# Expert stage in 64-row sub-tiles, two on TensorE's column halves, with expert weights in a ring; front and combine rearranged

## What is computed

```python
h = rmsnorm(x, norm1_w) * (1 + sc1) + sh1          # sh1, sc1, ... = split(silu(c) @ w_ada + b_ada, 6)
x = x + g1 * mixer(h)                              # includes the S5 scan and h @ w_gate
h = rmsnorm(x, norm2_w) * (1 + sc2) + sh2
# each row goes to 2 of 16 experts: the best group of 4, then the best two inside it
for e in range(16):
    he = silu(hf @ w_exp_gate[e]) * (hf @ w_exp_up[e])      # 1024 -> 256
    out = out + combine[:, e:e + 1] * (he @ w_exp_down[e])  # 256 -> 1024
y = rmsnorm(x + g2 * out, final_norm_w)
```

## Time and profile before

| | us |
|---|---|
| median of 3 runs | 2274.26 (2273.16 to 2274.49) |
| the profiled execution | 2273.5 |
| its span (first to last instruction) | 2270.9 |
| TensorE matmuls busy | 2074.7 (91%) |
| VectorE / ScalarE / POOL busy | 708.1 / 398.6 / 187.9 |
| moved by DMA | 245.71 MB |

### The profile page before, as it was taken

How to read it: one execution, slowest core, us unless ns; L and a number is a source line. 1 busy time by engine, 2 the same in 40 slices (tenths; PEclk the granted TensorE clock), 3 DMA queues, 4 the chain that set the end, 5 groups by cost and what they waited for, 6 DMA issues and landing times. The chain is left out here.

```text
span 2270.9 us, 26307 instructions
## 1 busy us (share of the span) xinstructions
PE 2074.7 (91%) x10412; PEld 1408.4 (62%) x10412; DVE 708.1 (31%) x1540; ACT 398.6 (18%) x851; POOL 187.9 (8%) x226
## 2 busy tenths in 40 slices
PE   6998499999989999997899999899999399999976
PEld 3674275654456665654789898566444388778852
DVE  3737701202052112333344444311232411111117
ACT  4220111003132001222212122300111111111102
POOL 2000000000000001210212121100000000000016
PEclk9999799999999999998999999999999599999988
DMA  8085331110021000110000000212200299999975
GB/s 283 30 145 204 130 89 37 41 37 0 0 52 29 28 28 20 37 37 1 19 11 11 1 11 19 95 42 102 88 38 28 79 358 345 357 354 352 353 245 190
DMA packets 187757, 245.71 MB, mean 108 GB/s; under 512 B 25583, under 2 KB 155143, under 8 KB 185575
## 3 DMA queue, kind: packets, MB, share of 16 engines
q1 hardware_dynamic: 179080, 214.51, 30.0%
q0 software_dynamic: 8592, 30.01, 3.7%
HBM read 212.28 MB, written 31.04 MB: 107 GB/s over the span
## 5 line engine op out<-in xcount | busy, mean ns | idle before, releaser
L2581 PEld LDWEIGHTS ex_ps<-ex_xt,ex_w_in 128*128 128x128 f32 x2048 | 235.1, 193 | 17.7 <-issue 14.8
L2581 PE MATMUL ex_ps<-ex_xt,ex_w_in 128*128 128x128 f32 x2048 | 235.4, 276 | 2.5 <-DMA ex_w_in<-in_w_exp_up 2.5
L1471 PE MATMUL cv_ps<-h,late 128*128 128x364 f32 (+1 forms) x576 | 179.0, 474 | 2.7 <-PEq L2821 2.7
L1471 PEld LDWEIGHTS cv_ps<-h,late 128*128 128x128 f32 x576 | 110.5, 193 | 70.4 <-issue 6.6
L2226 PE MATMUL pj_ps<-w_out,mix 128*128 128x512 f32 (+1 forms) x288 | 125.0, 593 | 2.8 <-PEq L2821 2.8
L2075 PE MATMUL go_ps<-h,out_w 128*128 128x364 f32 (+1 forms) x384 | 122.2, 473 | 4.1 <-PEq L2821 4.1
L2592 PE MATMUL ex_ps<-ex_w_down,ex_hid 128*128 128x512 f32 x256 | 118.2, 605 | 6.5 <-DVE ex_hid L2667 4.3
L1263 PE MATMUL gla_ps<-h,early 128*128 128x364 f32 (+1 forms) x384 | 120.7, 469 | 0.0
L459 PE MATMUL fr_ps<-h,fr_w_gate 128*128 128x364 f32 (+1 forms) x384 | 120.1, 471 | 0.0
L2075 PEld LDWEIGHTS go_ps<-h,out_w 128*128 128x128 f32 x384 | 73.8, 192 | 48.7 <-issue 5.6
L459 PEld LDWEIGHTS fr_ps<-h,fr_w_gate 128*128 128x128 f32 x384 | 72.1, 190 | 48.9 <-issue 7.6
(11 more groups left out here) (471 smaller groups left out, 2776.0 us busy)
## 6 DMA issues: line engine op xcount, KB each, us to landing
ex_w_in<-in_w_exp_gate SPq DMA_DIRECT2D x32, 1024.0 KB, 8.6
ex_w_in<-in_w_exp_up SPq DMA_DIRECT2D x32, 1024.0 KB, 11.2
ex_w_down<-in_w_exp_down SPq DMA_DIRECT2D x32, 1024.0 KB, 10.2
fr_y_cols<-in_w_ada SPq DMA_DIRECT2D x8, 2048.0 KB, 7.6
ys_dram<-ex_y SPq DMA_DIRECT2D x32, 512.0 KB, 10.1
late<-in_w_in SPq DMA_DIRECT2D x12, 512.0 KB, 4.4
glu_w_br<-in_w_ada SPq DMA_DIRECT2D x5, 1024.0 KB, 5.7
mix<-in_x_prompt SPq DMA_DIRECT2D x8, 512.0 KB, 10.8
```

Of the source, the lines that this page charges most:

```text
L1471: last = nc.tensor.matmul(ps[n][:, 0:width], g.cv_w(j % 2)[:, k], g.h[:, k, at:at + width], start=k == 0, stop=k == KD - 1)
L2581: last = nc.tensor.matmul(ps[2 + b][:, P * m:P * m + P], w_in[:, b, m // 2, k, P * (m % 2):P * (m % 2) + P], xt[:, b, k], start=m == 0 and ...
```

## The change

The expert stage is rewritten. The list is padded to 64 places for each expert instead of 128. There are 50 sub-tiles in 25 slots; sub-tile A of a slot uses columns 0 to 63 of TensorE's array and sub-tile B columns 64 to 127. The rows are now stationary (128x64) and the weights move (256 and 512 columns), and the matmuls of A and B alternate, each pair writing the two halves of the partitions of one PSUM bank. The product then has its rows on partitions and is transposed (two transposes and a copy) before down. Each expert's weights are loaded once, in order of experts, to a ring of four places; the first four loads stand in the route stage, later ones wait for the slot that last used the place. TensorE takes A's weights from the ring at an address from a register; B's are copied each slot to fixed buffers, by ScalarE (two of the eight row blocks of gate/up, and down) and VectorE (six row blocks). The y buffer is single and is stored from POOL's queue. POOL also makes the 18 diagonal matrices for the combine meanwhile. In the combine, VectorE adds to x instead of POOL. In the front, there are five slab buffers, all x tiles are turned before the first modulation, the placement in `s5_toeplitz` is issued by POOL, `EARLY` is 6, the late slabs are used at every second piece, and SP's order is changed.

The diff, cut to its core:

```diff
 # front
-        slabs = [glu_space[:, 0:2 * D], br_space[:, 0:2 * D], br_space[:, 2 * D:4 * D]]
+        slabs = [glu_space[:, 0:2 * D], br_space[:, 0:2 * D], br_space[:, 2 * D:4 * D], s_space[:, 2 * D:4 * D], b_space[:, 2 * D:4 * D]]
-        EARLY = 5
+        EARLY = 6
-            for l in range(LB):        # SP
-                sp.dma_start(g.s5_toeplitz[...], lags[:, :, 0:LB - l, :]).then_inc(placed, 16)
+            pool.wait_ge(lags_done, 1)  # POOL
+            for l in range(LB):
+                pool.dma_start(g.s5_toeplitz[...], lags[:, :, 0:LB - l, :]).then_inc(placed, 16)
+            late(1)
             gate_weights(2)
-            late(1)
             late(2)
             gate_weights(3)
             late(3)
             late(4)
             gate_weights(4)
             late(5)
-            late(6)
             gate_weights(5)
+            late(6)
             late(7)
+            gate_weights(6)
...
-            for i in range(5):
+            for i in range(NT):
                 turn_x(i)
             for k in range(4):
                 modulation(k)
-                turn_x(5 + k)
...
-                if q % 3:
-                    late(q - 1 - q // 3)
+                if q % 2 and q < 15 or q == 14:
+                    late(q // 2)
 # route
-            then(nc.vector.tensor_scalar(tiles[:, 0], total[:, NT], 0.0, None, ALU.is_gt))
-            for j in range(1, NT):
-                then(nc.vector.scalar_tensor_tensor(tiles[:, j % 2], total[:, NT], float(P * j), tiles[:, (j - 1) % 2], ALU.is_gt, ALU.add))
+            then(nc.vector.tensor_scalar(tiles[:, 0], total[:, NT], 1.0, float(SUB - 1), ALU.max, ALU.add))
+            then(nc.vector.tensor_copy(tiles_i[:, 0], tiles[:, 0]))
+            then(nc.vector.tensor_scalar(tiles_i[:, 1], tiles_i[:, 0], 6, None, ALU.logical_shift_right))
+            then(nc.vector.tensor_copy(tiles[:, 1], tiles_i[:, 1]))
+            for e in range(RING):      # SP, in the route stage
+                if e:
+                    sp.wait_ge(g.experts_loaded, 48 * e)
+                load_expert(sp, g, d, e)
 # experts, SP
+            for e in range(RING, NE):
+                after = sp.value_load(g.free_at[0:1, e - RING:e - RING + 1], min_val=2, max_val=2 * SLOTS)
+                sp.wait_ge(g.experts_loaded, 48 * e)
+                sp.wait_ge(S["down_psum"], after)
+                load_expert(sp, g, d, e)
 # experts, POOL
+            for s in range(SLOTS):
+                if s + 2 < SLOTS:
+                    pool.wait_ge(S["high_turned"], s + 1)
+                    gather(s + 2)
+                if 1 <= s <= NT:
+                    weights_of(s - 1)
+                pool.wait_ge(S["y_out"], 2 * s + 2)
+                pool.dma_start(g.ys_dram[P * s:P * s + P, :], y[:]).then_inc(S["stored"], 16)
 # experts, TensorE
+            def gate_up(s, place):
+                pe.wait_ge(S["xt_out"], 2 * s + 2)
+                pe.wait_ge(S["in_copied_act"], s + 1)
+                pe.wait_ge(S["in_copied_dve"], s + 1)
+                if s:
+                    pe.wait_ge(S["inner"], s)
+                for f, (bank, done) in enumerate(((gate_ps, "gate_psum"), (up_ps, "up_psum"))):
+                    for k in range(KD):
+                        own = g.ring[:, place, FF * (2 * k + f):FF * (2 * k + f) + FF].rearrange("p r f -> p (r f)")
+                        nc.tensor.matmul(bank[A, 0:FF], xt[:, s % 2, k, A], own, start=k == 0, stop=k == KD - 1, ...)
+                        last = nc.tensor.matmul(bank[B, 0:FF], xt[:, s % 2, k, B], lane_in[:, s % 2, k, f], start=k == 0, stop=k == KD - 1, ...)
+                    last.then_inc(S[done], 1)
+            def down(s, place):
+                ...
+                for c in range(2):
+                    for k in range(FF // P):
+                        nc.tensor.matmul(down_ps[c][A], inner_t[:, k, A], own, ...)
+                        last = nc.tensor.matmul(down_ps[c][B], inner_t[:, k, B], lane_down[:, k, 512 * c:512 * c + 512], ...)
+                    last.then_inc(S["down_psum"], 1)
+            for s in range(SLOTS):
+                place = bass.ds(pe.value_load(g.ring_of[0:1, 2 * s:2 * s + 1], min_val=0, max_val=RING - 1), 1)
+                need = pe.value_load(g.need[0:1, 2 * s:2 * s + 1], min_val=48, max_val=48 * NE)
+                pe.wait_ge(g.experts_loaded, need)
+                gate_up(s, place)
+                if s + 1 < SLOTS:
+                    turn_low(s + 1)
+                turn_inner(s)
+                if s + 1 < SLOTS:
+                    turn_high(s + 1)
+                down(s, place)
 # experts, ScalarE
+            for s in range(SLOTS):
+                copy_down(s, place)
+                if s + 1 < SLOTS:
+                    place = place_of(s + 1)
+                    copy_in(s + 1, place)
+                ...
 # experts, VectorE
+            for s in range(SLOTS):
+                if s:
+                    store_half(s - 1)
+                if s + 1 < SLOTS:
+                    copy_in(s + 1)
+                ...
 # combine
-                pool.wait_ge(S["gated"], 2 * i + 2)
-                nc.gpsimd.tensor_tensor(x1[0:n, i], x1[0:n, i], gated[0:n, i % 2], ALU.add).then_inc(S["added"], 1)
+                dve.wait_ge(S["gated"], 2 * i + 2)
+                nc.vector.tensor_tensor(x1[0:n, i], x1[0:n, i], gated[0:n, i % 2], ALU.add).then_inc(S["added"], 1)
```

More of the change, by code:

```diff
@@ L163, in stage_front @@
         x_in = [sem(f"x_in{i}") for i in range(NT)]
-        slab_in = [sem(f"slab_in{b}") for b in range(3)]
+        slab_in = [sem(f"slab_in{b}") for b in range(5)]
         pad_zero = sem("pad_zero")
@@ L2427, in _ @@
             groups, experts = g.logits[:, :, 0:NG], g.logits[:, :, NG:]
-            then(nc.vector.tensor_tensor_scan(count[:], g.ones[:, 0:MT], g.ones[:, 0:MT], 0.0, ALU.mult, ALU.add))
+            then(nc.vector.tensor_tensor_scan(count[:], g.ones[:, 0:SUBS], g.ones[:, 0:SUBS], 0.0, ALU.mult, ALU.add))
             then(nc.vector.tensor_scalar(rank[:], count[:, 0:NE], -1.0, NE + 1.0, ALU.mult, ALU.add))
@@ new lines, in weights_of @@
+            def weights_of(i):
+                n = P if i < NT - 1 else DEC
+                for k in range(2):
+                    nc.gpsimd.tensor_scalar(g.diag(i, k)[0:n, 0:n], g.ident[0:n, 0:n], g.choice_w[0:n, k, i:i + 1], None, ALU.mult).then_inc(g.diag_made, 1)
+            gather(0)
+            gather(1)
+            for s in range(SLOTS):
[6 more added lines that the diff above has]
+                pool.dma_start(g.ys_dram[P * s:P * s + P, :], y[:]).then_inc(S["stored"], 16)
@@ L2585, in down, with turn_low @@
-            def down(t, b, rounds, freed):
-                pe.wait_ge(down_loaded[b], rounds)
-                pe.wait_ge(S["hid"], t + 1)
-                if freed is not None:
-                    pe.wait_ge(S["y_out"], freed)
+            def turn_low(s):
+                pe.wait_ge(x_loaded[s % 2], 16 * (s // 2 + 1))
+                if s:
+                    pe.wait_ge(S["xt_out"], 2 * s)
+                for k in range(4):
+                    last = nc.tensor.transpose(low_ps[:, P * k:P * k + P], x[:, s % 2, P * k:P * k + P], g.ident[:])
+                last.then_inc(S["low_turned"], 1)
@@ L2611, in _ @@
-            down(t, 0, 8 * MT, 2 * t - 2)
-            gate_up(t + 1, 1, 16 * MT, t)
-            down(t + 1, 1, 8 * MT, 2 * t)
+                        at = 2 * KD * FF + D * k + 512 * c
+                        own = g.ring[:, place, at:at + 512].rearrange("p r f -> p (r f)")
+                        nc.tensor.matmul(down_ps[c][A], inner_t[:, k, A], own, start=k == 0, stop=k == FF // P - 1, skip_group_check=True)
+                        last = nc.tensor.matmul(down_ps[c][B], inner_t[:, k, B], lane_down[:, k, 512 * c:512 * c + 512], start=k == 0,
+                                                stop=k == FF // P - 1, skip_group_check=True)
@@ L2714, in stage_combine @@
         rstd = sb("rstd", [P, NT])
-        S = {n: sem(n) for n in "gathered0 gathered1 gathered2 gains_loaded weights psum gated added ssq std rstd y stored".split()}
+        S = {n: sem(n) for n in "gathered0 gathered1 gathered2 gains_loaded psum gated added ssq std rstd y stored".split()}
         gathered = [S[f"gathered{b}"] for b in range(3)]
@@ L2735, in _ @@
                 gather(i)
[L2736 to L2741 removed]
+            for i in range(3, NT):
+                gather(i)
         @block.sync
@@ L2765, in _ @@
                     for k in range(2):
-                        last = nc.tensor.matmul(ps[2 * (i % 2) + c][0:n], weights[0:n, i % 2, k, 0:n], rows[0:n, i % 3, k, 512 * c:512 * c + 512],
+                        last = nc.tensor.matmul(ps[2 * (i % 2) + c][0:n], g.diag(i, k)[0:n, 0:n], rows[0:n, i % 3, k, 512 * c:512 * c + 512],
                                                 start=k == 0, stop=k == 1)
@@ L2780, in _ @@
         def _(dve):
-            def weigh(i):
-                n = size(i)
-                if i >= 2:
```

(4 more changed lines are left out.)

354 lines of the change are left out of this document (166 added, 188 removed).

## The result

The changed kernel takes 2182.35 us (median, 2181.19 to 2188.91), the kernel before 2274.02 in the same comparison: a ratio of 0.960, 95% interval 0.958 to 0.962, 92 us less. The forecast was 2176 in 2157 to 2248. The profiled execution took 2183.2 us with a span of 2181.4, 89.5 less than before.

| from one event to the next (us) | before | after | gain | forecast |
|---|---|---|---|---|
| start to the gated linear unit (front) | 346.70 | 331.83 | 14.87 | 14.5 |
| to the last logits (unchanged stages) | 1427.30 | 1424.57 | 2.73 | 0 |
| to the first listing product (route) | 19.91 | 18.75 | 1.16 | 1.1 |
| to the end of `row_token` | 8.59 | 8.53 | 0.06 | 0 |
| to the first gather of rows | 1.00 | 10.39 | **-9.39** | 0 |

The account below looks back on a forecast made before the run. TensorE was taken to set the experts' pace, loads just keeping up. Gains 69.3 (experts) + 1.65 (route, start) + 12 (combine) + 14.5 (front) = 97.4 us, from 2273.5 to 2176 us, range 2157 to 2248.

Parts of the forecast that it names:

- Halves: Experts, TensorE: matmul pairs alternating between the two column halves overlap at half price, 0.1105 us per 256-column record.
- one after the other: Rival, gate/up and down pairs: the halves run serially, 10.5 us more a slot, total 2440 us; chance 0.06.
- overlap in part: Rival, expert pairs: 1.25 passes each, 2.6 us more a slot, total 2242 us; chance 0.18, shared with a late copy.
- The slot: Experts: 25 slots of 12.45 us each replace 32 tiles; gain 69.3 us, bounds 85 and 43.
- The chain: Experts, between gate/up and down: product, two transposes, PSUM copy and four hops take 1.71 us, against 1.0 to 1.2 before.
- The DMA share: Experts: loads fall from 96 to 48 MB, 141 of 313 us at 340 GB/s; share near 0.5, off the path.
- Registers: Rival, experts: run-time addresses of 20 matmuls a slot cost 152 us if none were hidden, total 2328 us; chance 0.04.
- The copies: Experts, B's weights: ScalarE 1.9 + 1.0 us and VectorE 2.3 us a slot, covered by gate/up.
- Route and start: Route compares -1.1 us, first gate/up -1.55 us, last store some 1 us slower: net gain 1.65, bounds 0 and 3.
- The last store: End of the experts: POOL's issue of the last y store is some 1 us slower.
- Combine: VectorE's period falls from 5.53 to 4.08 us with the add on VectorE: gain 12 us, bounds 6 (late gathers) and 14.
- Front: EARLY=6 moves a gate column into the 27.08 us scan wait: gain 14.5 us, bounds 5 and 17; failure rival 2186 us, 0.10.

Follow-up runs that it names:

- my experiment: The changed kernel with the last of the 25 stores of expert outputs issued by SyncE instead of GpSimd: 2180.36 us, ratio 0.959.
- GpSimd experiment: The changed kernel with the combine's residual addition on GpSimd again, its weights still made beforehand: 2192.69 us.
- gains experiment: The changed kernel with three route loads, last store on SyncE, and the combine's gains and norm weights loaded one slot before the experts end: 2166.99 us.
- the kernel with seven columns: The changed kernel with seven gate columns ahead of the S5 outputs instead of six (EARLY = 7): 2192.8 us in one execution.
- blocks of two: The changed kernel with gate and up products in the order A, A, B, B instead of A, B: 2182.98 us.

## Why the forecast held, step by step

**Halves.** Half price for alternating pairs was taken from the S5 inputs, 136 columns wide; it holds at 256 columns (0.216 us a pair) and at 512 (down's 16 records, 6.9 us at 0.434 each, take 3.65 with their drain). The rivals "one after the other" and "overlap in part" had no share. The figure of the Trainium skill's TensorE: Matmul & The Clock Gate, section Part 3: Packing small matmuls, that I had set against it (2.38 for three column tiles), does not carry over to two halves: measured, two.

**The slot.** 12.45 forecast, 12.24 measured; the gain of 69.3 became 72.3. The chain was right to 0.02 us, the pairs 2% cheaper than the line between two full-width forms. The first slot took 2.7 us more than the others, where 1.5 were forecast. The DMA share was 0.59 and not near 0.5: the 141 us of loads left out the gathers and the y stores (and took 1 MB as 10^6 bytes; with the 3.15 MB of one expert's three matrices it is 148). Registers cost nothing that shows: pairs follow each other without gaps. The copies are covered, as costed (1.76 to 1.99 us on VectorE, 2.3 in the sum; 1.9 and 1.05 on ScalarE).

**Route and start.** Here the sum failed. Compares (1.16) and start (1.56) are right, but the step on the loads ("They now wait on SP for the down of the slot that frees a place") looked only at the experts. The first four loads I moved into the route's block without costing their queue: 3 MB at a time, each waiting for the one before, 11.05 us apart, so SyncE reaches the barrier 9.2 us after the list is ready. I had read them only as weights that are there in time, and left out that the block ends with its slowest engine. Part of the price was to be had from rows of before: three experts are 9.44 MB, 27.8 us at 340 GB/s. With two figures of after, 2.5 us for the fourth's issue (1790.46 to 1792.93) and 26.4 from the first load to the list, that is 30.3 us against 26.4, 4 us late. Measured, it was 9.2, since a load whose landing is waited for takes 11.05 us and not 9.25.

**The last store.** "POOL's issue of the last store is some 1 us slower" named the right instruction and priced the wrong thing. From the end of the issue to the first gather pass 7.6 us on GpSimd and 3.3 on SyncE, for the same 512 KB. The landing is not the difference (2.9 and 2.6 us from the start of the issue), though my experiment was built on it, and its 4.45 us came out right by luck. The term that was missing is GpSimd's DRAIN behind the last store: 4.16 us in all seven kernels that store from GpSimd to the end, 4.07 and off the path in the four others, 0.007 on SyncE. Why it takes that long stays open. Of 25 stores only the last is exposed.

**Combine.** 12 and 12.2, for the reason given: 9.7 of it is the addition (GpSimd experiment). What comes next was named as a bound, late gathers: in tiles four to eight TensorE's products begin 0.1 us after their second gather has landed, VectorE's period is 4.2 us on average instead of 4.08, with 4.9 once, and the gains experiment shows DMA as the limit at its start.

**Front.** 14.5 and 14.87. The waits for gate weights are 4.22 and 4.31 us (forecast 4 for two columns), those for slabs fell from 10.1 to 2.7. TensorE was ready at 274.9, not 271: after each of the waits it ran a piece at a lower clock, 7.72 and 7.41 us instead of 5.1, which I had not counted. Of the 6.87 us that were left, ScalarE's copies need 5.5, as the kernel with seven columns shows, so the cover was 1.4 us and not 6.

**Unchanged stages.** 2.73 us of the gain in the profiles is not the change's but the luck of one execution; without it the sum would have been 10.7 us too high. These stages took 1424.5 to 1424.6 us in seven of the profiles and 1427 to 1428 in four, among them that of the kernel before, at a lower granted clock in one or two places. What brings the clock down there, with TensorE busy, stays open.

## What to carry to other kernels

Work that is moved to an earlier stage must be costed to the end of its issue: a block ends when its slowest queue has issued, and a queue that waits for one transfer before it starts the next is slow by the transfers, not by the instructions. Of a long row of hidden stores the last one is on the path, and behind it whatever its queue does to close the block: here that cost 4.16 us on GpSimd and 0.007 on SyncE, while the landing was the same to 0.3 us. And two 64-column halves are worth two passes as long as the order in the program alternates within a few records.

## What the hardware did that was not expected

- GpSimd's DRAIN at the end of the experts took 4.07 to 4.16 us, after its last store had landed, in every kernel run here whose y stores it issues; no busy time shows it.
- TensorE brings products on the two column halves side by side even when four records of the same half stand in a row; with sixteen in a row only three at each border overlap. The Trainium skill's TensorE: Matmul & The Clock Gate, section Part 3: Packing small matmuls, says that matmuls start and end strictly in program order. The rows with blocks of two, where records of A and B start in turn 0.06 us apart, don't agree with that, and the measurement decides here.
- A wait of 4 us on TensorE costs more than itself: the piece behind it took 7.4 to 7.7 us instead of 5.1, at a granted clock of 0.66 to 0.69 in that stretch, against 1.00 in the next one (between the 1.2 and the 2.4 GHz levels):

```profile
...
184.00:191.80 7.80, 7.71 (x19) 4.35 (x22) 5.72 (x25) 0.00 (x0) 0.00 (x0) 0.66 0.01 2
194.40:204.30 9.90, 9.90 (x34) 6.00 (x32) 7.29 (x32) 0.56 (x1) 0.00 (x0) 1.00 0.74 265
...
```
